# Gates of the recurrent mixer as two 64-row float32 products per unit

## The chip, the cores and the metric

The program runs on one core of one Trainium2 chip. The metric is the device time of one execution in microseconds, as the median of several executions. A profiled execution of the same program is read beside it: its span, from the first to the last instruction, and the instructions of the five engines (TensorE as PE, its weight loads as PEld, VectorE as DVE, ScalarE as ACT, GpSimd as POOL, and SyncE as SP, which here only issues transfers).

## What is computed

Two layers of a diffusion backbone with 256 latent tokens and 256 context tokens, 1024 wide. Each layer is a half-step SwiGLU block, a token mixer, and another half-step SwiGLU block, each behind an RMSNorm whose shift, scale and gate come from a conditioning vector. The change lies in the mixer. Its recurrent half has 8 heads of 64 channels, and its gates are block-diagonal products, one 64 by 64 matrix for each head, direction and kind:

```
def rglru_coeffs(xc, w_r, b_r, w_i, b_i, lam):
    xh = xc.reshape(bsz, n, LRU_HEADS, LRU_HEAD_DIM)
    r = jax.nn.sigmoid(jnp.einsum("bnhd,hde->bnhe", xh, w_r).reshape(bsz, n, LRU_WIDTH) + b_r)
    i = jax.nn.sigmoid(jnp.einsum("bnhd,hde->bnhe", xh, w_i).reshape(bsz, n, LRU_WIDTH) + b_i)
    log_a = (-RG_C * r * jax.nn.softplus(-lam)).astype(jnp.float32)
    a = jnp.exp(log_a)
    b = jnp.sqrt(-jnp.expm1(2.0 * log_a)) * (i * xc).astype(jnp.float32)
    return a, b
```

The scan `h = a * h + b` then runs forward and backward over latent and context tokens, and its sum is multiplied by a GELU branch. The other half of the mixer is a spatial gating block. Both halves feed one output projection.

## The kernel before

Channels lie on the 128 partitions and tokens on the free axis, 512 columns for both streams. The large weights come as 320 slots of 128 x 1024 float32 values through a ring of four slots (`raw`, `w_hi`, `w_lo`). ACT copies each slot into its rounded high part (`split_hi`, L877), DVE subtracts that from the original (`split_lo`, L1174), and PE makes three reduced-precision products for each block of 128 x 128 (`product`, L437): high by high, high by low, low by high. A slot q + 4 is split when slot q is done, so ACT and DVE have about three slots of room.

The mixer's `in_stage` has 16 slots, q = 0 to 15. Slots 0 to 3 give the recurrent input `xc` (ACT L1041, then a convolution on DVE, L1410), 4 to 7 the values of the spatial block (L718 to L720), 8 to 11 the GELU branch `gl`, 12 to 15 its multiplier. After each of the slots 3 to 10 PE computes one **unit** u = 0 to 7 of gates: channel tile t = u // 2 (two heads, 128 channels) and direction d = u % 2. A unit has two results in two banks of PSUM, for the kinds r and i.

The weights of a unit and a kind are a 128 x 128 matrix with two blocks of 64 x 64 on its diagonal and zeros elsewhere. They lie in `bd`, which is laid over the ring `ada_raw`, and POOL writes the zeros (`zero_blocks`). In layer 0 weights and `xc` are split in high and low parts as well: ACT L1035 and L1018, DVE L1553 and L1419, and PE makes three products for each kind (L747). In layer 1 PE takes the float32 operands as they are (L749), which the trace shows as two records for each product.

Behind a unit ACT reads the banks: a tanh of r into `l_q` (L1075), a tanh of i into `l_bx` (L1076, which signals `ti_ready`), an exponential into `l_a` (L1079) and a tanh into `l_s` (L1081). After units 3 and 7 it takes the square roots of four units (L1087), which needs another function table. DVE forms the coefficients (L1426, L1429) and after the roots the scans (L1438 to L1449). ACT may start unit 4 only when the first pair of scans is done, since `l_q` and the others have four buffers.

What orders the engines around it: PE's unit u waits for `ti_ready` of unit u - 1 in layer 0 (one pair of banks) and u - 2 in layer 1 (two pairs). Every engine runs its list in the order written, so a wait holds all that is queued behind it: on PE the next slots. The end of the mixer in layer 1 hangs on the last scans, on GELU (L1091), on the split of y (L1105, L1479), and on the output slots that take it.

## Time and profile before

| | us |
|---|---|
| median of 3 runs | 1577.48 |
| lowest and highest | 1576.68, 1584.05 |
| span of the profiled execution | 1575.5 |
| PE busy | 1561.2 (99%) |
| DVE busy | 1001.6 (64%) |
| ACT busy | 631.0 (40%) |
| POOL busy | 82.5 (5%) |

The median is 2.0 us above the profiled span. A busy share is a mean over stages; ACT at 40% is nearly full in one of them. Ends of matmuls are modelled, so the pace of PE is read from the starts of its records: the three-product stream of 512 columns has a start every 0.23 us.

### The profile page before, as it was taken

Reading aid. Unit: us, or ns where it says so; the run is one execution under the profiler, and the core shown is the slowest. Engines: PE = TensorE matmul, PEld = TensorE weight load, DVE = VectorE, ACT = ScalarE, POOL = GpSimd, SP = SyncE. Lnnn points to the kernel's source line nnn. Section 1 sums busy time; section 2 is a strip of 40 time slices with the busy share of each in tenths; the row PEclk is TensorE's granted clock in tenths of the full one; section 3 lists DMA queues with packets and bytes.
Section 4 is the critical chain, followed back from the end, with each engine's and each line's share of the span. In section 5 each row is a group of like instructions: output and inputs, shape, how many; then the busy total and the mean of one; then the engine's idle time right before and its main releaser. Section 6 shows DMA issues by size and latency. Waiting matters only on the chain.

```text
span 1575.5 us, 22302 instructions
## 1 busy us (share of the span) xinstructions
PE 1561.2 (99%) x9052; PEld 1338.1 (85%) x9052; DVE 1001.6 (64%) x1243; ACT 631.0 (40%) x856; POOL 82.5 (5%) x100
## 2 busy tenths in 40 slices
PE   8999999999999999999999999999999999999998
PEld 6888888888988888888888898888888897999998
DVE  5776773783967577777364267777445358975554
ACT  4433322332784343323222243333232249764553
POOL 0000000011100200000000100000000111000001
PEclk9999999999999999999999999999999999999999
DMA  9565553653322355565353336556354323456563
GB/s 365 201 197 179 186 162 119 208 192 94 115 75 79 94 166 193 176 201 173 107 196 99 107 121 201 193 183 195 100 173 148 107 91 108 147 188 197 190 203 117
DMA packets 71786, 249.95 MB, mean 159 GB/s; under 512 B 11664, under 2 KB 11920, under 8 KB 70672
## 3 DMA queue, kind: packets, MB, share of 16 engines
q1 hardware_dynamic: 71696, 248.70, 48.1%
q8 instruction: 62, 1.02, 0.3%
q14 instruction: 28, 0.23, 0.1%
HBM read 247.62 MB, written 1.05 MB: 158 GB/s over the span
## 4 chain that ended last, share of the span: by engine, by line
PE 96%; DVE 2%; ACT 1%; issue 0%; POOL 0%; POOLq 0%; DVEq 0%; ACTq 0%
PE bank L437 85%; PE bank L574 2%; PE bank L580 2%; PE bank L576 2%; PE bank L452 1%; PE bank L475 1%; PE bank L747 1%; PE bank L720 1%; PE bank L718 1%; PE bank L719 1%; PE bank L749 0%; PE bank L468 0%; DVE w_lo L1174 0%; PE bank L529 0%; PE bank L460 0%
## 5 line engine op out<-in xcount | busy, mean ns | idle before, releaser
L877 ACT ACTIVATE w_hi<-raw 128x1024 fp32r<-128x1024 f32 x317 | 335.9, 1060 | 807.0 <-PE bank L437 792.8
L1174 DVE TENSOR_TENSOR w_lo<-raw,w_hi 128x1024 fp32r<-128x1024 f32 x317 | 387.7, 1225 | 371.9 <-ACT w_hi L877 371.6
L437 PE MATMUL bank<-z_hi,w_hi 128*128 128x512 f32 (+1 forms) x1480 | 535.9, 362 | 2.4 <-DVE w_lo L1174 1.9
L437 PE MATMUL bank<-z_lo,w_hi 128*128 128x512 f32 (+1 forms) x1480 | 532.1, 360 | 0.0
L437 PE MATMUL bank<-z_hi,w_lo 128*128 128x512 f32 (+1 forms) x1480 | 531.9, 359 | 0.0
L437 PEld LDWEIGHTS bank<-z_hi,w_hi 128*128 128x128 f32 x1480 | 278.0, 188 | 49.7 <-DVE w_lo L1174 3.2
L437 PEld LDWEIGHTS bank<-z_hi,w_lo 128*128 128x128 f32 x1480 | 278.0, 188 | 42.6
L437 PEld LDWEIGHTS bank<-z_lo,w_hi 128*128 128x128 f32 x1480 | 278.1, 188 | 42.6 <-issue 1.0
L437 PE MATMUL bank<-h_hi,w_hi 128*128 128x512 f32 (+1 forms) x770 | 266.5, 346 | 0.0
L437 PE MATMUL bank<-h_lo,w_hi 128*128 128x512 f32 (+1 forms) x770 | 265.7, 345 | 0.0
L437 PE MATMUL bank<-h_hi,w_lo 128*128 128x512 f32 (+1 forms) x770 | 265.6, 345 | 0.0
L1349 DVE SCALAR_TENSOR_TENSOR up_acc<-ada_raw,c_cols,up_acc 128x1024 f32<-128x1024 f32 x168 | 208.0, 1280 | 3.5 <-ACT up_acc L977 2.4
L437 PEld LDWEIGHTS bank<-h_hi,w_hi 128*128 128x128 f32 x770 | 145.0, 188 | 19.3 <-issue 1.2
L437 PEld LDWEIGHTS bank<-h_hi,w_lo 128*128 128x128 f32 x770 | 145.0, 188 | 18.1
L437 PEld LDWEIGHTS bank<-h_lo,w_hi 128*128 128x128 f32 x770 | 145.1, 188 | 18.0
L1373 DVE TENSOR_TENSOR scr<-scr,bank 128x512 f32<-128x512 f32 (+1 forms) x88 | 54.6, 620 | 81.9 <-PE bank L437 81.6
L1701 POOL TENSOR_TENSOR scr<-scr 128x512 f32<-128x512 f32 (+1 forms) x29 | 47.6, 1641 | 776.0 <-ACT scr L891 776.0
L1187 DVE SCALAR_TENSOR_TENSOR res<-bank,gates,res 128x256 f32<-128x256 f32 x80 | 35.7, 479 | 66.1 <-PE bank L437 66.1
L1349 DVE SCALAR_TENSOR_TENSOR down_acc<-ada_raw,c_cols,down_acc 128x1024 f32<-128x1024 f32 x56 | 75.0, 1381 | 0.6 <-ACT down_acc L977 0.4
L925 ACT ACTIVATE z_hi<-scr,n_shift 128x256 fp32r<-128x256 f32 x88 | 42.8, 506 | 50.0 <-DVE scr L1273 50.0
L574 PE MATMUL bank<-z_hi,w_hi 128*128 128x256 f32 x208 | 56.4, 286 | 0.8 <-ACT z_hi L925 0.7
L576 PE MATMUL bank<-z_hi,w_lo 128*128 128x256 f32 x208 | 55.5, 282 | 0.0
(185 smaller groups left out, 1234.3 us busy)
## 6 DMA issues: line engine op xcount, KB each, us to landing
raw<-weights SPq DMA_DIRECT2D x320, 512.0 KB, 4.1
ada_raw<-ada_w SPq DMA_DIRECT2D x128, 512.0 KB, 4.2
ada_head<-head_w SPq DMA_DIRECT2D x8, 1024.0 KB, 18.5
res<-x_t SPq DMA_DIRECT2D x4, 512.0 KB, 4.8
ada_raw<-gate_w SPq DMA_DIRECT2D x4, 256.0 KB, 5.3
ws<-sgu_w SPq DMA_DIRECT2D x2, 256.0 KB, 4.0
bs<-sgu_b SPq DMA_DIRECT2D x2, 256.0 KB, 4.2
out<-final SPq DMA_DIRECT2D x2, 256.0 KB, 3.0
```

Of the source, the lines that this page charges most:

```text
L437: m = pe.matmul(bank[:, to], w, x[:, k, at], start=start and i == 0, stop=stop and i == 2, skip_group_check=True)
L452: m = pe.matmul(p_ada[32 * j:32 * j + 32, i * 256:i * 256 + 256], sel[:, st, :], w[:, st, :, j, :], start=(st == 0), stop=(st == 1), tile_ ...
L574: pe.matmul(banks[q][:, COLS[s]], w_hi[:, q, c], z_hi[:, k, z], start=(k == 0 and s == 0), stop=False, skip_group_check=True)
L576: pe.matmul(banks[q][:, COLS[s]], w_lo[:, q, c], z_hi[:, k, z], start=False, stop=False, skip_group_check=True)
L580: m = pe.matmul(banks[q][:, COLS[s]], w_hi[:, q, c], z_lo[:, k, z], start=False, stop=last, skip_group_check=True)
L877: act.activation(w_hi[:, r, :], raw[:, r, :], ACT.Copy).then_inc(hi_ready, 1)
L925: act.activation(z_hi[:, k, row_cols(n, s)], scr[:, k % 3, COLS[s]], ACT.Identity, bias=n_shift[:, n, k, s:s + 1]).then_inc(z_hi_ready, 1)
L1174: dve.tensor_tensor(w_lo[:, r, :], raw[:, r, :], w_hi[:, r, :].bitcast(F32), ALU.subtract).then_inc(lo_ready, 1)
L1187: m = dve.scalar_tensor_tensor(res[:, d, COLS[s]], tail_bank(d, s, n)[:, COLS[s]], gates[:, n - 1, d, s:s + 1], res[:, d, COLS[s]], ALU.mu ...
L1349: dve.scalar_tensor_tensor(acc[:, st, :], ada_raw[:, u % ADA_RING, :], c_cols[:, k, st:st + 1], acc[:, st, :], ALU.mult, ALU.add).then_inc ...
L1373: dve.tensor_tensor(scr[:, 2, 0:w], scr[:, q // 2, 0:w], pa[q][:, 0:w], ALU.mult).then_inc(hid_ready, 1)
L1701: pool.tensor_tensor(scr[:, 2, 0:w], scr[:, 2, 0:w], scr[:, d % 2, 0:w], ALU.add).then_inc(sqsum_ready, 1)
```

## The change

In both layers a unit's gates become two float32 products of 64 rows each. Each takes one head (64 of the 128 partitions of `xc`), and its 64 x 128 weights hold that head's r and i blocks side by side. The two products sit at row positions 0 and 64 of the array and write one bank each. The first bank then holds r of head 0 on partitions 0 to 63 and i on 64 to 127, the second i of head 1 on 0 to 63 and r on 64 to 127. So ACT reads each kind in two halves of 64 partitions: four tanh activations for a unit where there were two, with a third row of `half_b` for the shifted bias.

The splits of weights and of `xc` in layer 0, the zero blocks and their semaphores go. The weights come in four transfers for each layer in place of two, with the same bytes.

```
-                        if l == 0:
-                            pe.wait_ge(split_lo_ready, LT + t_ + 1)
-                        for kind_, dst in enumerate(gate_banks(l, u)):
-                            b = kind_ * 8 + d_ * 4 + t_
-                            if l == 0:
-                                for i, (w, x) in enumerate(((bd_high, xc_high), (bd_high, xc_low), (bd_low, xc_high))):
-                                    m = pe.matmul(dst[:], w[:, b, :], x[:, t_ % 2, :], start=(i == 0), stop=(i == 2))
-                            else:
-                                m = pe.matmul(dst[:], bd[:, b, :], xc[:, t_, :], start=True, stop=True)
+                        for a, dst in enumerate(gate_banks(l, u)):
+                            own = slice(64 * a, 64 * a + 64)
+                            m = pe.matmul(dst[:], bd[own, d_ * 4 + t_, :], xc[own, t_, :], start=True, stop=True,
+                                          tile_position=(64 * a, 0))
                         m.then_inc(gate_mm, 1)
...
-                        act.activation(l_q[:, r, :], g_r[:], ACT.Tanh, bias=half_b[:, 0, c:c + 1], scale=0.5).then_inc(act_chain, 1)
-                        act.activation(l_bx[:, r, :], g_i[:], ACT.Tanh, bias=half_b[:, 1, c:c + 1], scale=0.5).then_inc(ti_ready, 1)
+                        act.activation(l_q[low, r, :], first[low, :], ACT.Tanh, bias=half_b[low, 0, c:c + 1], scale=0.5)
+                        act.activation(l_q[high, r, :], second[high, :], ACT.Tanh, bias=half_b[high, 0, c:c + 1],
+                                       scale=0.5).then_inc(act_chain, 1)
+                        act.activation(l_bx[low, r, :], first[high, :], ACT.Tanh, bias=half_b[high, 2, c:c + 1], scale=0.5)
+                        act.activation(l_bx[high, r, :], second[low, :], ACT.Tanh, bias=half_b[low, 2, c:c + 1],
+                                       scale=0.5).then_inc(ti_ready, 1)
...
-                if l == 0:
-                    for t in range(LT):
-                        act.activation(bd_high[:, t::LT, :], bd[:, t::LT, :], ACT.Copy).then_inc(split_hi_ready, 1)
...
-            def gate_lo(t):
-                dve.tensor_tensor(xc_low[:, t % 2, :], xc[:, t, :], xc_high[:, t % 2, :].bitcast(F32),
-                                  ALU.subtract).then_inc(split_lo_ready, 1)
...
-                link(pool.memset(bd[0:64, :, 64:P], 0.0))
-                pool.memset(bd[64:P, :, 0:64], 0.0).then_inc(bd_zero, 1)
```

PE in layer 0, from the end of slot 3 over unit 0 into slot 4, before:

```order
1824 L437 MATMUL bank<-z_hi,w_lo 128x512
1825 L747 MATMUL bank<-xc_high,bd_high 128x512
1826 L747 MATMUL bank<-xc_low,bd_high 128x512
1827 L747 MATMUL bank<-xc_high,bd_low 128x512
1828 L747 MATMUL bank<-xc_high,bd_high 128x512
1829 L747 MATMUL bank<-xc_low,bd_high 128x512
1830 L747 MATMUL bank<-xc_high,bd_low 128x512
1831 L718 MATMUL bank<-w_hi,z_hi 128x512
```

The same place after the change (`ada_raw` is the tile over which `bd` lies):

```order
1824 L427 MATMUL bank<-z_hi,w_lo 128x512
1825 L732 MATMUL bank<-xc,ada_raw 128x512 x2
1826 L708 MATMUL bank<-w_hi,z_hi 128x512
1827 L709 MATMUL bank<-w_hi,z_lo 128x512
1828 L710 MATMUL bank<-w_lo,z_hi 128x512
```

Six products of a unit are now two, at the same place between the slots. In layer 1 there were two and are two.

ACT in layer 1, from slot 8's weight split over unit 4 to the start of unit 5, before:

```order
505 L877 ACTIVATE w_hi<-raw 128x1024
506 L1075 ACT_TABLE_LOAD
507 L1075 ACTIVATE l_q<-bank,half_b 128x512
508 L1076 ACTIVATE l_bx<-bank,half_b 128x512
509 L1079 ACTIVATE l_a<-l_q,lam_t 128x512
510 L1081 ACTIVATE l_s<-l_q,lam_t 128x512
511 L1048 ACTIVATE gl<-bank 128x256
512 L877 ACTIVATE w_hi<-raw 128x1024
513 L1060 ACTIVATE v_n<-bank,tok,tokr 128x512 x2
514 L1075 ACTIVATE l_q<-bank,half_b 128x512
```

And after:

```order
524 L861 ACTIVATE w_hi<-raw 128x1024
525 L1044 ACT_TABLE_LOAD
526 L1044 ACTIVATE l_q<-bank,half_b 64x512
527 L1045 ACTIVATE l_q<-bank,half_b 64x512
528 L1047 ACTIVATE l_bx<-bank,half_b 64x512
529 L1048 ACTIVATE l_bx<-bank,half_b 64x512
530 L1052 ACTIVATE l_a<-l_q,lam_t 128x512
531 L1054 ACTIVATE l_s<-l_q,lam_t 128x512
532 L1020 ACTIVATE gl<-bank 128x256
533 L861 ACTIVATE w_hi<-raw 128x1024
534 L1028 ACTIVATE v_n<-bank,tok,tokr 128x512 x2
535 L1044 ACTIVATE l_q<-bank,half_b 64x512
```

Each unit has two activations more on ACT, all four ahead of `ti_ready`; nothing else moved there.

## Rows read from the trace of the kernel before

**Rows 1.** The page: busy time, and the chain that ended last by engine.

```profile
PE 1561.2 (99%) x9052; PEld 1338.1 (85%) x9052; DVE 1001.6 (64%) x1243; ACT 631.0 (40%) x856; POOL 82.5 (5%) x100
...
PE 96%; DVE 2%; ACT 1%; issue 0%; POOL 0%; POOLq 0%; DVEq 0%; ACTq 0%
```

**Rows 2.** Chain in layer 1's mixer: start, length, what (us); a part of its pieces.

```profile
1319.72 1.73 PE bank L749 x4
1321.48 0.69 ACT l_q L1075
...
1347.70 1.28 ACT L1087
...
1358.04 4.22 PE bank L437 x31
```

**Rows 3.** PE's timeline: start, length, engine, line, operation, count; layer 0, unit 0.

```profile
419.68 0.39 PE L747 MATMUL bank<-xc_high,bd_high 128*128 128x512 f32 x1
...
421.06 0.39 PE L718 MATMUL bank<-w_hi,z_hi 128*128 128x512 f32 x1
```

**Rows 4.** PE's timeline, layer 1: units 0 and 6.

```profile
1306.10 1.88 PE L749 MATMUL bank<-xc,ada_raw 128*128 128x512 f32 x4
...
1308.05 0.40 PE L719 MATMUL bank<-w_hi,z_lo 128*128 128x512 f32 x1
...
1333.49 1.95 PE L749 MATMUL bank<-xc,ada_raw 128*128 128x512 f32 x4
```

**Rows 5.** PE's timeline around a sum that uses four column strips at once (L452).

```profile
142.99 0.39 PE L437 MATMUL bank<-z_hi,w_lo 128*128 128x512 f32 x1
143.31 1.93 PE L452 MATMUL bank<-up_acc,sel 128*32 128x256 f32 x32
...
145.51 0.40 PE L437 MATMUL bank<-z_lo,w_hi 128*128 128x512 f32 x1
```

**Rows 6.** The same line up to 143.35 and up to 143.65: count, ns, first to last start.

```profile
L452 PE MATMUL bank<-up_acc,sel x4: 403/403/403, 143.3 to 143.3; 128*32 128x256 f32 x4
...
L452 PE MATMUL bank<-up_acc,sel x8: 379/391/403, 143.3 to 143.6; 128*32 128x256 f32 x8
```

**Rows 7.** ACT's timeline, layer 1: unit 0, a wait, and unit 4.

```profile
1308.40 0.68 ACT L1075 ACTIVATE l_q<-bank,half_b 128x512 f32<-128x512 f32 x1
1308.97 0.70 ACT L1076 ACTIVATE l_bx<-bank,half_b 128x512 f32<-128x512 f32 x1
1309.54 0.83 ACT L1079 ACTIVATE l_a<-l_q,lam_t 128x512 f32<-128x512 f32 x1
1310.25 0.82 ACT L1081 ACTIVATE l_s<-l_q,lam_t 128x512 f32<-128x512 f32 x1
1310.96 1.06 ACT L877 ACTIVATE w_hi<-raw 128x1024 fp32r<-128x1024 f32 x1
1312.50 0.69 ACT L1075 ACTIVATE l_q<-bank,half_b 128x512 f32<-128x512 f32 x1 [0.49 <-PE bank L749]
...
1328.83 0.38 ACT L1048 ACTIVATE gl<-bank 128x256 f32<-128x256 f32 x1 [0.22 <-PE bank L437]
1329.11 1.05 ACT L877 ACTIVATE w_hi<-raw 128x1024 fp32r<-128x1024 f32 x1
```

**Rows 8.** ACT's timeline, layer 0: slot 6, units 3 and 4.

```profile
440.38 1.06 ACT L877 ACTIVATE w_hi<-raw 128x1024 fp32r<-128x1024 f32 x1 [2.69 <-PE bank L720]
441.76 0.69 ACT L1075 ACTIVATE l_q<-bank,half_b 128x512 f32<-128x512 f32 x1 [0.32 <-PE bank L747]
...
453.49 0.68 ACT L1076 ACTIVATE l_bx<-bank,half_b 128x512 f32<-128x512 f32 x1
```

**Rows 9.** Chain in layer 0's mixer: PE between slot 8 and unit 5.

```profile
454.26 1.63 PE bank L747 x6
```

**Rows 10.** Stretches at the end: busy PE, PEld, DVE, ACT, POOL, granted clock, DMA.

```profile
1571.00:1574.00 3.00, 0.00 (x0) 0.00 (x0) 0.45 (x1) 0.00 (x0) 0.81 (x1) 1.00 0.88 334
1574.00:1575.50 1.50, 0.00 (x0) 0.00 (x0) 0.00 (x0) 0.00 (x0) 0.00 (x0) 0.64 0.04 14
```

More of the change, by code:

```diff
@@ L47 @@
 GATE_LAG = 3
-GATE_HIGH_AT = (1, 2, 5, 7)
-GATE_LOW_AT = (0, 1, 5, 7)
 SIDE = 3
@@ L179, in build @@
         l_a = sb("l_a", [P, 4, T])
-        with ExitStack() as gate_scope:
-            sb("y_lru_first", [P, 2, T], F32, gate_scope)
-            xc_high = sb("xc_high", [P, 2, T], F32R, gate_scope)
         y_lru = sb("y_lru", [P, LT, T])
-        with ExitStack() as gate_scope:
-            sb("gl_first", [P, 2, T], F32, gate_scope)
-            xc_low = sb("xc_low", [P, 2, T], F32R, gate_scope)
         gl = sb("gl", [P, LT, T])
@@ L191, in build @@
         v_n = sb("v_n", [P, 4, 512])
-        with ExitStack() as gate_scope:
-            bd_high = sb("bd_high", [P, 16, P], F32R, gate_scope)
         y_sgu = sb("y_sgu", [P, LT, T])
@@ L196, in build @@
         xc = sb("xc", [P, LT, T])
-        bd_low = sb("bd_low", [P, 16, P], F32R)
+        sb("y_alone_rest", [P, 16, P])
         ws = sb("ws", [P, LT, P])
@@ L403, in _ @@
                             for a in range(2):
-                                sp.dma_start(bd[64 * a:64 * a + 64, :, 64 * a:64 * a + 64], gate_w[l, a]).then_inc(bd_in, 16)
+                                for kind in range(2):
+                                    c = 64 * (kind ^ a)
+                                    sp.dma_start(bd[64 * a:64 * a + 64, :, c:c + 64],
+                                                 gate_w[l, a][:, 8 * kind:8 * kind + 8, :]).then_inc(bd_in, 16)
                     if f == 0:
@@ L1011, in down_stage @@
                 norm(n, at["slot"] + DOWN_SLOTS)
-            def gate_hi(t):
-                if t >= 2:
-                    act.wait_ge(gate_mm, 2 * (t - 1))
-                act.wait_ge(xc_ready, t + 1)
-                act.activation(xc_high[:, t % 2, :], xc[:, t, :], ACT.Copy).then_inc(split_hi_ready, 1)
             def weight_ahead(slot, i):
@@ L1048, in in_stage @@
                         act.activation(gl[:, t, 0:wl], po[t % 2][:, 0:wl], ACT.Copy).then_inc(copy_ready, 1)
-                    if l == 0 and q == GATE_HIGH_AT[0]:
-                        gate_hi(0)
                     split_hi(at["slot"] + q + 4, q % 4)
-                    if l == 0 and q in GATE_HIGH_AT[1:]:
-                        gate_hi(GATE_HIGH_AT.index(q))
                     if q == 2:
@@ L1068, in in_stage @@
                         r = u % 4
-                        g_r, g_i = gate_banks(l, u)
+                        first, second = gate_banks(l, u)
+                        low, high = slice(0, 64), slice(64, P)
                         act.wait_ge(gate_mm, 8 * l + u + 1)
@@ L1549, in in_stage @@
                 m4 = wl // P
-                if l == 0:
-                    for t in range(LT):
-                        dve.wait_ge(split_hi_ready, t + 1)
-                        dve.tensor_tensor(bd_low[:, t::LT, :], bd[:, t::LT, :], bd_high[:, t::LT, :].bitcast(F32),
-                                          ALU.subtract).then_inc(split_lo_ready, 1)
                 for q in range(12):
@@ L1562, in in_stage @@
                     split_lo(s, q % 4)
-                    if l == 0 and q in GATE_LOW_AT:
-                        gate_lo(GATE_LOW_AT.index(q))
                     for u in {3: (0,), 4: (1,), 5: (2,), 6: (3,), 9: (4, 5), 10: (6,), 11: (7,)}.get(q, ()):
@@ L1640, in softplus @@
                 dve.tensor_scalar(half_b[:, 0, :], par[:, C_BR:C_BR + DEPTH * 2 * LT], 0.5, None, ALU.mult)
-                dve.tensor_scalar(half_b[:, 1, :], par[:, C_BI:C_BI + DEPTH * 2 * LT], 0.5, None, ALU.mult).then_inc(lam_ready, 1)
+                for a in range(2):
+                    of, to = slice(64 * a, 64 * a + 64), slice(64 - 64 * a, P - 64 * a)
+                    m = dve.tensor_scalar(half_b[to, 2, :], par[of, C_BI:C_BI + DEPTH * 2 * LT], 0.5, None, ALU.mult)
+                m.then_inc(lam_ready, 1)
             dve.memset(eps, EPS)
@@ L1754, in _ @@
                 norm(3 * l + 1)
-                zero_blocks(l)
+                zero_pads(l)
                 prep_gate(l, 1)
```

19 lines of the change are left out of this document (5 added, 14 removed).

## The prediction

> **What bounds the kernel now.** I read the page first: PE is busy 99% of the span and makes 96% of the chain that ended last [rows 1]. The reader should see that a stretch is in general worth what it takes on PE. Then I read the chain inside the two mixers, since the change lies only there. In layer 0 it is PE throughout, but for one short wait. In layer 1 it leaves PE: after unit 3 [rows 2] it runs over ACT and DVE (tanh, exponential, table load, scans), through units 5, 6 and 7 on ACT, over the last table load, until PE starts the output slots at 1358.04. From unit 3 on, layer 1's mixer is bound by ACT, and PE waits for it: unit 6 begins at 1333.49, only when unit 4's second tanh is read [rows 4]. So the change must be costed on two engines.
>
> **PE's part.** In layer 0 a unit takes six starts, 419.68 to 421.06: 1.38 us [rows 3]. In layer 1 it begins at 1306.10, and slot 4's second product begins at 1308.05; less the 0.23 us of its first that is 1.72 us, or 0.43 for each of four records [rows 4]. After the change both layers have two products of two records. If the two row positions run beside each other, that is 2 x 0.43 = 0.86 us.
>
> No row has row positions. The nearest are the sums over four column strips, also float32: four records start within 143.3, and the next four by 143.6, though each product has two records of its own [rows 6]. So strips do run beside each other, and products that are written one behind the other do not hold each other up. All 32 records and the way in and out take from 142.99 to 145.51, less two products of 0.23: 2.06 us [rows 5]. The strips' own pace is some 0.216 for four records, 8 x 0.216 = 1.73, so the change of shape costs 0.33 us for each visit. A gate's weights are four times wider than a strip's, and their load (an estimate: half of the 0.23 us pitch that a load and a product share in the stream, 0.11) is laid bare once more or not at all: a unit costs 0.86 + 0.33 to 0.44, and I take 1.25 us. The bounds are 0.86 (no cost of shape) and 1.72 + 0.4 = 2.1 (nothing beside anything). Against before that is -0.13 us for each unit in layer 0 and -0.47 in layer 1.
>
> By the Trainium skill, "TensorEngine Tiling (Array Packing)", Key Properties, a change of tiling mode drains TensorE; by that rule the 0.33 would be found here too, and rows 5 agree with it. "TensorE: Matmul & The Clock Gate", Part 3, The mechanism, speaks against this change in another way: products start and end in strict order. That is a rival below, worked out from rows.
>
> **ACT's part.** Each unit has two tanh activations more. Neighbouring ones of 128 x 512 start 0.57 us apart (1308.40, 1308.97, 1309.54), the exponential and the second tanh take 0.70 each [rows 7]. No row has 64 partitions. The lower bound is an activation with the same number of elements, 128 x 256, of which `gl` starts 0.28 ahead of the next [rows 7]; the upper bound is 0.57, where only columns count. I take 0.57, since the 512 columns stay and 128 partitions already run side by side. "ScalarE: Activation LUTs" of the Trainium skill gives one element per cycle and lane, so it too would leave the 0.57. A unit thus costs ACT 2 x 0.57 = 1.14 us more, all of it ahead of `ti_ready`, and behind it queue the exponential, the next weight split and the next unit.
>
> **Layer 1.** ACT needs 0.95 (weight split, 1310.96 to its successor) + 4 x 0.57 + 1.40 = 4.63 us for a unit; PE's period would fall from 4.49 to 4.02 us (2.77 for the slot plus 1.25). So ACT becomes the bound from unit 0 and PE's gain there is worth nothing. Walk ACT from 1308.40, where unit 0 starts as before. It has no wait left: unit 3, 3 x 4.64 later, starts at 1322.32, against 1321.48 [rows 2]; +0.84. Units 3 to 7 then add 5 x 1.14 = 5.70. All of the chain to 1358.04 hangs on that, except that ACT had waited 0.28 us for POOL's statistics ahead of unit 5, which now is ready first. Sum +6.26 us. DVE and the weights are not late: slot 15's high part would be made about 1350 and is wanted about 1359. PE would lie idle some 6 us ahead of unit 6 (due at 1330.5, released at 1336.6), 2 ahead of unit 7 and 2.7 ahead of the spatial products behind slot 12.
>
> That idle time could cost clock. At the end of this kernel PE has nothing from 1571 on, and the granted clock falls within 1574 to 1575.5 (0.64 there) [rows 10]. If it falls here, unit 6 and slot 10 at half pace take 8.3 us in place of 4.1 and end 2.1 us after the release of unit 7. ACT wants unit 7's gates only at 1350.1, some 5 us later, so I cost it at nothing; the cover is ACT's own lateness.
>
> **Layer 0.** ACT's 4.64 us a unit lie under PE's period of 6.8, with one exception. Units 4 to 7 reuse buffers, so between unit 3 and unit 5 the chain is: slot 6 done, unit 3 on ACT, table load, roots, scans, table load, unit 4's tanhs, then PE's unit 5. Before, unit 5 began at 454.26 [rows 9] with 0.41 us of wait (unit 4's second tanh began at 453.49 [rows 8]). Now unit 3's gates are ready 4 x 0.13 = 0.5 us earlier, and ACT, which had waited 0.32 for them behind its weight split [rows 8], starts earlier by as much. Units 3 and 4 add 1.14 each. Unit 5 begins at 454.26 - 0.5 + 2.28 = 456.04; PE was there at 453.2, so it waits 2.8 us. Units 5, 6 and 7 give back 3 x 0.13. Layer 0 ends +1.4 us; with units of 0.86 us it would be -0.8, with 2.1 us +7.4.
>
> **Edits that cost and bring nothing.** The eight weight and input splits on ACT and the eight on DVE lay ahead of unit 5's chain or beside PE's products; PE waited for none of them, and ACT, early once, waits for PE by unit 1. POOL's zeros were beside PE too. Eight weight transfers in place of four add two issues of about 0.4 us to SP's queue for each layer, ahead of a weight slot that is wanted a slot time (5 us) later. Without that cover they would cost under 1 us.
>
> **Sum.** 6.3 + 1.4 = 7.7 us, on a profiled span of 1575.5: 1583.2. The median was 2.0 above the span, so 1585.2 us, 0.49% above 1577.48. A measurement of this kernel tells about 0.5% (7.9 us) from no change, so the forecast sits on the bound itself.
>
> **Rivals.** *Strict order.* If the second product's first record waits for the first product's second, three passes replace two: 3 x 0.43 + 0.39 = 1.68 us. Layer 1 keeps its 6.3; in layer 0 unit 5's chain is late by 4 x 0.30 + 2.28 and three units add 0.9: +4.4. Total +10.7: 1588.2. Rows 6 speak against it.
>
> *Nothing beside anything.* Units of 2.1 us: +7.4 in layer 0, and in layer 1 a PE period of 4.87 us above ACT's makes unit 3 later by another 0.7: +6.9. Total +14.3: 1591.8. That would also be the change not doing what it says.
>
> *Free shape.* Units of 0.86: 6.3 - 0.8 = +5.5, 1583.0. Rows 5 speak against it.
>
> *Half activations cost half.* If 64 x 512 takes 0.28 us, ACT has nothing more to do. Then unit 3 starts 4 x 0.47 = 1.9 us early in layer 1, and layer 0 gains 0.5 + 3 x 0.13: -2.8 us, 1574.7. The sign turns at about 0.35 us for a half activation. Even with free shape it would be some -7. Nothing in the profile has this form.
>
> *Clock in layer 0.* If PE's wait of 2.8 us ahead of unit 5 lets the clock fall, what follows is PE-bound; a few us at half pace add about 3: 1588.2.
>
> **How the numbers follow.** Forecast 0.60 (its own range 1583.5 to 1587, from 1 us either way for the walk), strict order 0.10, nothing beside 0.10, free shape 0.10, half activations 0.06, clock 0.04. Predicted is the forecast, 1585.2. The range 1581.5 to 1591 leaves out the half activations and nothing beside (0.16). The forecast's 0.60 splits evenly at the bound of 7.9 us: within 0.5% are 0.30 of it, free shape and most of half activations, 0.45; slower is the other 0.30 with three rivals, 0.53; faster 0.02.
>
> **What would show it.** In the new trace: gate records in pairs that start together, two pairs 0.43 us apart, and a unit of 1.2 to 1.3 us; tanh rows of 0.57 pitch with 64 partitions; ACT without a wait from 1308 to the last roots in layer 1; PE idle about 6 us ahead of unit 6 and 2.8 ahead of layer 0's unit 5; the output slots of layer 1 beginning 7.7 us later in the span. A shorter half activation, or units 6 and 7 released on time, would make it wrong.

## The result, and the profile after

The changed kernel takes 1598.03 us (median of 4 runs, 1595.9 to 1602.72) where the kernel before takes 1577.51: 1.0121 times as long, 95% interval 1.0096 to 1.0146. The forecast was 1585.2 us, its range ended at 1591. The profiled execution has a span of 1597.0 us, 1.8 below its own time of 1598.8.

The page after, to set beside [rows 1]: busy time, and the chain that ended last by engine.

```profile
PE 1568.5 (98%) x9036; PEld 1335.8 (84%) x9036; DVE 997.8 (62%) x1236; ACT 651.0 (41%) x880; POOL 80.5 (5%) x96
...
PE 93%; ACT 4%; DVE 1%; DMA 1%; issue 1%; SPq 0%; POOLq 0%; DVEq 0%; ACTq 0%
```

ACT has 20 us more work, and its part of the chain has gone from 1% to 4%. PE's timeline in layer 0 (start, length, engine, line, operation, count), the answer to [rows 3]:

```profile
420.77 0.39 PE L427 MATMUL bank<-z_hi,w_lo 128*128 128x512 f32 x1
421.09 1.13 PE L732 MATMUL bank<-xc,ada_raw 64*128 64x512 f32 x4
422.15 0.50 PE L708 MATMUL bank<-w_hi,z_hi 128*128 128x512 f32 x1
422.48 0.39 PE L709 MATMUL bank<-w_hi,z_lo 128*128 128x512 f32 x1
```

From 420.77 to 422.48 less two products of 0.23 a unit takes 1.25 us, as forecast. Its records up to 421.5 and up to 422 (count, duration in ns, first and last start):

```profile
L732 PE MATMUL bank<-xc,ada_raw x2: 694/694/694, 421.1 to 421.1; 64*128 64x512 f32 x2
...
L732 PE MATMUL bank<-xc,ada_raw x4: 589/642/694, 421.1 to 421.6; 64*128 64x512 f32 x4
```

The first records of both products start together (0.006 us apart in the trace), and the second ones 0.53 us later. ACT's timeline of a unit in layer 1, the answer to [rows 7]:

```profile
1314.87 1.06 ACT L861 ACTIVATE w_hi<-raw 128x1024 fp32r<-128x1024 f32 x1
1315.82 0.67 ACT L1044 ACTIVATE l_q<-bank,half_b 64x512 f32<-64x512 f32 x1
1316.51 0.68 ACT L1045 ACTIVATE l_q<-bank,half_b 64x512 f32<-64x512 f32 x1
1317.21 0.68 ACT L1047 ACTIVATE l_bx<-bank,half_b 64x512 f32<-64x512 f32 x1
1317.91 0.68 ACT L1048 ACTIVATE l_bx<-bank,half_b 64x512 f32<-64x512 f32 x1
1318.62 0.81 ACT L1052 ACTIVATE l_a<-l_q,lam_t 128x512 f32<-128x512 f32 x1
```

The half tanhs start 0.70 us apart where whole ones start 0.57 apart. From the first tanh to the exponential 2.80 us pass, before 1.14: 1.66 more, not 1.14. PE then waits in layer 0 for unit 5 and in layer 1 for unit 6 (PE's timeline, with the idle time before a row and who ended it):

```profile
457.93 2.08 PE L732 MATMUL bank<-xc,ada_raw 64*128 64x512 f32 x4 [3.07 <-ACT l_bx L1048]
459.94 0.79 PE L427 MATMUL bank<-z_hi,w_hi 128*128 128x512 f32 x1
460.53 0.63 PE L427 MATMUL bank<-z_lo,w_hi 128*128 128x512 f32 x1
460.96 0.63 PE L427 MATMUL bank<-z_hi,w_lo 128*128 128x512 f32 x1
...
1346.49 2.08 PE L732 MATMUL bank<-xc,ada_raw 64*128 64x512 f32 x4 [8.06 <-ACT l_bx L1048]
```

Both times a unit takes 2.08 us, and in layer 0 the products behind it start 0.43 us apart in place of 0.23: TensorE is at its lower level, 1.2 GHz. The stretches (busy PE, PEld, DVE, ACT, POOL, granted clock, DMA) show the fall:

```profile
450.00:457.00 7.00, 4.86 (x22) 3.67 (x20) 6.90 (x10) 4.51 (x6) 0.00 (x0) 1.00 0.14 42
457.00:464.00 7.00, 6.07 (x14) 3.73 (x15) 6.21 (x12) 6.88 (x11) 3.62 (x4) 0.52 0.09 35
1338.00:1341.00 3.00, 0.43 (x4) 0.22 (x2) 2.90 (x5) 3.00 (x6) 0.00 (x0) 1.00 0.00 0
1341.00:1351.50 10.50, 5.01 (x18) 3.54 (x19) 10.29 (x16) 9.43 (x14) 4.08 (x6) 0.52 0.17 53
```

A third wait, of 3.7 us, stands ahead of the spatial products behind slot 12 of layer 1 (forecast: 2.7), and behind it the granted clock is 0.66 once more, from 1364 to 1369.

And there is a loss that no step of the prediction names. PE's main line in the last down stage, 1520 to 1560 us of each trace, before (L437) and after (L427): count, duration in ns, first and last start.

```profile
L437 PE MATMUL bank<-h_lo,w_hi x119: 276/276/276, 1519.8 to 1559.9; 128*128 128x256 f32 x119
```

```profile
L427 PE MATMUL bank<-h_hi,w_hi x99: 280/284/284, 1524.4 to 1559.6; 128*128 128x256 f32 x99
```

Before, 119 starts of one of the three kinds fill 40.1 us, one product every 0.1133 us. After, 99 fill 35.2 us (98 steps of three), one every 0.120.

Setting the k-th product of one trace against the k-th of the other shows where the time was lost. The table does that for all kernels of this study: how many us PE falls behind the kernel before in each stretch (named by the time in the trace of before; gate products and the throwaway ones of e6 left out).

| | to 100 | 100-405 | layer 0 mixer, 405-510 | 510-1305 | layer 1 mixer, 1305-1400 | 1400-end | all |
|---|---|---|---|---|---|---|---|
| after | 0.55 | 0.77 | 5.33 | 0.77 | 10.51 | 3.49 | 21.42 |
| e1 layout only | -0.22 | 0.78 | 0.23 | 0.75 | 0.10 | 3.49 | 5.13 |
| e2 old layout | -0.22 | 0.01 | 3.84 | -0.01 | 10.00 | 0.00 | 13.62 |
| e3 half tanhs | 0.23 | 0.00 | 5.59 | 0.01 | 11.30 | 0.00 | 17.13 |
| e4 whole tanhs | 0.52 | -0.01 | -1.24 | 0.00 | -2.05 | 0.00 | -2.78 |
| e5 halves by group | 1.02 | 0.00 | 2.93 | -0.02 | 9.36 | 6.52 | 19.81 |
| e6 kept busy | 1.58 | 0.00 | 2.40 | 0.03 | 10.05 | 0.00 | 14.06 |
| e7 column 96 | 1.02 | 0.77 | 0.25 | 0.76 | 0.31 | 5.02 | 8.13 |
| e8 shift 128 | -0.54 | 2.78 | 0.47 | 6.28 | -0.23 | 6.52 | 15.28 |
| e9 square tiles | -0.26 | 0.00 | 5.04 | 0.03 | 1.23 | 6.51 | 12.55 |
| e10 shift 256 | 1.56 | 0.00 | -0.03 | 0.01 | 0.14 | 6.52 | 8.20 |
| e11 by output | -0.19 | 0.00 | 2.41 | 0.05 | 10.44 | 0.00 | 12.71 |
| e12 four quarters | 0.54 | 0.00 | -1.55 | 0.01 | 2.83 | 0.00 | 1.83 |
| e13 layer 0 alone | 0.32 | 0.00 | -1.55 | 0.00 | 0.00 | 0.00 | -1.23 |
| e14 plus 2 units | 0.78 | 0.00 | -1.54 | 0.04 | -1.01 | 0.00 | -1.73 |
| e15 plus 4 units | 1.47 | 0.00 | -1.54 | 0.05 | -0.91 | 6.51 | 5.58 |

The first column is chance, the arrival of the first weights. On some chips part of the executions of every kernel, the kernel before too, run all 256-column products from 1400 on at 0.118 us and end 6.5 us later (the 6.5 in the last column); where a time below is called undisturbed, these are left out.

### The profile page after: what moved, and what is told of

The parts are those of the page before. It is cut to its first block, busy times and chain, and to the rows that moved or that the text cites. A ratio compares the mean times of both kernels' runs of the same rounds, so it can differ in the third digit from the quotient of the medians.

```text
span 1597.0 us, 22281 instructions
## 1 busy us (share of the span) xinstructions
PE 1568.5 (98%) x9036; PEld 1335.8 (84%) x9036; DVE 997.8 (62%) x1236; ACT 651.0 (41%) x880; POOL 80.5 (5%) x96
## 3 DMA queue, kind: packets, MB, share of 16 engines
q8 instruction: 62, 1.02, 0.3%
## 4 chain that ended last, share of the span: by engine, by line
PE 93%; ACT 4%; DVE 1%; DMA 1%; issue 1%; SPq 0%; POOLq 0%; DVEq 0%; ACTq 0%
PE bank L427 84%; PE bank L564 2%; PE bank L570 2%; PE bank L566 2%; DMA ada_head<-head_w 1%; PE bank L442 1%; ACT w_hi L861 1%; ACT l_q L1045 0%; PE bank L519 0%; ACT l_bx L1048 0%; ACT l_q L1044 0%; ACT l_a L1052 0%; PE bank L732 0%; PE bank L708 0%; PE bank L743 0%
## 5 line engine op out<-in xcount | busy, mean ns | idle before, releaser
L427 PE MATMUL bank<-z_hi,w_hi 128*128 128x512 f32 (+1 forms) x1480 | 538.4, 364 | 1.9 <-DVE w_lo L1147 1.4
L427 PE MATMUL bank<-z_lo,w_hi 128*128 128x512 f32 (+1 forms) x1480 | 535.2, 362 | 0.0
L427 PE MATMUL bank<-z_hi,w_lo 128*128 128x512 f32 (+1 forms) x1480 | 534.9, 361 | 0.0
L427 PEld LDWEIGHTS bank<-z_hi,w_hi 128*128 128x128 f32 x1480 | 280.4, 189 | 55.1 <-issue 10.2
L427 PEld LDWEIGHTS bank<-z_hi,w_lo 128*128 128x128 f32 x1480 | 280.1, 189 | 42.8
L427 PEld LDWEIGHTS bank<-z_lo,w_hi 128*128 128x128 f32 x1480 | 280.3, 189 | 41.5
L427 PE MATMUL bank<-h_hi,w_hi 128*128 128x512 f32 (+1 forms) x770 | 268.7, 349 | 0.0
L427 PE MATMUL bank<-h_hi,w_lo 128*128 128x512 f32 (+1 forms) x770 | 268.3, 348 | 0.0
L427 PE MATMUL bank<-h_lo,w_hi 128*128 128x512 f32 (+1 forms) x770 | 266.9, 347 | 0.0
L427 PEld LDWEIGHTS bank<-h_lo,w_hi 128*128 128x128 f32 x770 | 145.4, 189 | 19.6
L427 PEld LDWEIGHTS bank<-h_hi,w_hi 128*128 128x128 f32 x770 | 145.6, 189 | 19.2 <-issue 1.2
L427 PEld LDWEIGHTS bank<-h_hi,w_lo 128*128 128x128 f32 x770 | 145.5, 189 | 19.1
```

The costliest lines, as they stand in the source:

```text
L427: m = pe.matmul(bank[:, to], w, x[:, k, at], start=start and i == 0, stop=stop and i == 2, skip_group_check=True)
```

## Experiments

**e1 and e2: the layout.** The third row of `half_b` makes that tile 64 bytes longer in each partition, and all tiles allocated behind it (`h_hi`, `h_lo`, `y_hi` and the mixer's) stand 64 bytes further on. e1 puts that alone into the kernel before, e2 takes it alone out of the changed one.

```
-        half_b = sb("half_b", [P, 2, DEPTH * 2 * LT])
+        half_b = sb("half_b", [P, 3, DEPTH * 2 * LT])
```

> The kernel before with one row more in half_b (three in place of two, the third unused), as the change has it. Nothing else differs; every tile that is allocated behind half_b lies 64 bytes further on. Layout theory: the four down stages run at the slower pace seen in the changed kernel (256-column products every 0.120 us in place of 0.113 in the last one, 512-column ones every 0.229 in place of 0.227 in the other three), which is 528 products x 0.006 = 3.1 us plus some 0.8 for each of three: +5.5 us, 1583. Rival, that the pace came from the gates or from a fallen clock: no difference, 1577.5.

> The changed kernel, but the shifted bias goes to the unused row 1 of half_b, so that half_b keeps two rows and all tiles lie where they lay before. Layout theory: 5.5 us less than the changed kernel, about 1592.5, with 0.113 us between products in the last down stage. Rival: 1598 as the changed kernel, with 0.120 there.

e1 took 1583.09 us, 1.0033 times before (1.0021 to 1.0044), with nothing computed otherwise. e2 took 1591.41 (1.0084, 1.0067 to 1.0101). Last down stage of e1, same view as above:

```profile
L437 PE MATMUL bank<-h_hi,w_lo x112: 283/283/283, 1519.8 to 1559.8; 128*128 128x256 f32 x112
```

112 where 119 fitted. So 5.5 us of the loss are the layout: 3.5 in the last down stage, the rest nearly all in the three down stages of 512 columns, where a product takes 0.229 us in place of 0.227. (The 256-column products of those three stages give a little back: 0.115 to 0.117 in place of 0.119.) Only stages whose moving operand is a shifted tile are slower.

**e3 and e4: tanhs against products.** e3 has the kernel before's products and layout with each tanh in two halves. e4 is e2 with two whole tanhs; on half of the partitions it takes the one gate for the other, so its output isn't the reference's, but every engine has the instructions of the change with whole tanhs.

```
-                        act.activation(l_q[:, r, :], g_r[:], ACT.Tanh, bias=half_b[:, 0, c:c + 1], scale=0.5).then_inc(act_chain, 1)
...
+                        for to, bank, row, ready in ((l_q, g_r, 0, act_chain), (l_bx, g_i, 1, ti_ready)):
+                            for a in range(2):
+                                own = slice(64 * a, 64 * a + 64)
+                                m = act.activation(to[own, r, :], bank[own, :], ACT.Tanh, bias=half_b[own, row, c:c + 1],
+                                                   scale=0.5)
+                            m.then_inc(ready, 1)
```

> The kernel before (products, splits and layout as before) with each of a unit's two tanhs made in two halves of 64 partitions, the same partitions in bank and tile. If a half takes 0.70 us from start to start wherever it reads, as in the changed kernel, a unit costs ACT 1.66 us more: in layer 1 unit 3 starts 2.4 us late and five units add 8.3, +10.5 us; in layer 0 units 3 and 4 add 3.3, and a wait of that length may cost clock, up to 3.4 more: 1591 to 1595. Rival, that 0.70 belongs to reading the banks of row products or to crossing partitions, and a plain half takes 0.57: +1.14 a unit, some +8.5 us, 1586.

> The changed kernel in the old layout, with the two tanhs of a unit taken over all 128 partitions, the first bank to l_q and the second to l_bx. It leaves out the sorting of r and i by head, so the gates are mixed up; every other instruction is there. It is the products' part alone. My walk says: units of 1.25 us, layer 1's chain starts 1.9 us early and layer 0 gains 0.9: -2.7 us, 1574.8, and the clock never falls in the mixers. Rival, that the 64-row products cost something beyond their own time: 1577.5 or more.

e3: 1594.3 us (1.0101, 1.0084 to 1.0118). e4: 1574.25 (0.9977, 0.9967 to 0.9987). The halves alone cost 16.7 us; the products alone bring 3.4. Both signs are thus shown apart: the edit that the change is named after is a gain, what it forces on ACT is five times that.

**e5 and e11: why 0.70.** e5 is e3 with the four halves ordered by partitions, `l_q` low, `l_bx` low, `l_q` high, `l_bx` high. e11 puts the same order of outputs into e2, where the two kinds of one head come from opposite halves of a bank.

> The kernel before with its own gate products and layout, and each tanh in two halves of 64 partitions, now ordered by partitions: l_q low, l_bx low, l_q high, l_bx high. So of the two steps between neighbouring halves of a unit that e3 had from low to high, and the one back, the middle one is now the only change of partitions; the steps from a half to the next on the same 64 partitions are two. Theory A (any ScalarE activation on 64 partitions costs 0.70 us, as the 0.70 between starts in e3): the starts stay 0.70 us apart everywhere and the time is that of e3, 1594.3 +- 1.5 us. Theory B (the 0.13 us over the 0.57 of a whole tanh come from the change of partitions): two of the four starts are 0.57 us apart, a unit costs about 0.26 us less in ScalarE, 8 units of layer 1 save 2.1 us, and the time is about 1592; if the write of one half is also what the next waits for, more.

> e2 (the change with the old layout) with the four half tanhs of a unit in another order: l_q low, l_bx low, l_q high, l_bx high, by the partitions that they write. Within each pair the tanh reads the other 64 partitions than the one ahead of it, but writes the same; between the pairs it reads the same and writes others. Theory A (the 0.12 us on top of a start come where the written partitions change, as in e5 from low to high): two of the four distances are 0.57 us, 8 units of layer 1 save 2 us, 1589 us. Theory B (they come where the partitions that are read change): only the middle distance and none of the pairs' is 0.57 us, about 1 us saved, 1590.4. Theory C (where either changes): 0.70 everywhere, 1591.4 as e2. Nothing is left out.

ACT's timeline in layer 1, e5 and then e11:

```profile
1317.37 0.69 ACT L1077 ACTIVATE l_q<-bank,half_b 64x512 f32<-64x512 f32 x1
1317.96 0.67 ACT L1080 ACTIVATE l_bx<-bank,half_b 64x512 f32<-64x512 f32 x1
1318.64 0.68 ACT L1077 ACTIVATE l_q<-bank,half_b 64x512 f32<-64x512 f32 x1
1319.23 0.67 ACT L1080 ACTIVATE l_bx<-bank,half_b 64x512 f32<-64x512 f32 x1
1319.92 0.81 ACT L1085 ACTIVATE l_a<-l_q,lam_t 128x512 f32<-128x512 f32 x1
```

```profile
1315.86 0.67 ACT L1044 ACTIVATE l_q<-bank,half_b 64x512 f32<-64x512 f32 x1
1316.54 0.69 ACT L1045 ACTIVATE l_bx<-bank,half_b 64x512 f32<-64x512 f32 x1
1317.23 0.68 ACT L1046 ACTIVATE l_q<-bank,half_b 64x512 f32<-64x512 f32 x1
1317.94 0.68 ACT L1048 ACTIVATE l_bx<-bank,half_b 64x512 f32<-64x512 f32 x1
1318.65 0.82 ACT L1052 ACTIVATE l_a<-l_q,lam_t 128x512 f32<-128x512 f32 x1
```

In e5 the distances are 0.59, 0.68, 0.59, 0.69: a half costs nearly what a whole one costs (0.57) when it follows one on the same partitions, and 0.1 us more when the partitions change. In e11 the second half writes the same partitions as the first and reads others: 0.68. The third writes others: 0.69. So a change on either side is enough, theory C. In layer 1's mixer e5 loses 9.36 us where e3 loses 11.30, close to the 2.1 that theory B of e5 expected. e5 took 1590.6 us undisturbed (four runs, 1588.8 to 1592.8), e3 1594.3, of which a part is a fall of the clock in layer 0 that e5's trace does not have. Two runs of e11, the profiled one first, took 1590.1 and 1590.9, like e2; the other two took 1594.4 and 1599.4, and without their traces it stays open what they lost. "VectorE: DVE Perf Modes" of the Trainium skill, section "Two Vector instructions with no wait between them", has this rule for VectorE: an instruction is held until all earlier ones have finished when an input or the output starts in another group of 32 partitions than the last one's. These rows show the same pattern on ScalarE (0.59 against 0.68), and every half tanh of the change but the first of a unit is such a case.

The traces of e3 and e5 show one case more. The last half of a unit there reads the high partitions of a bank and the next unit's first half the low ones. Three activations lie between them, but none reads a bank. The distance from the weight split to that first half is 1.07 us (in e3 from 1318.47 to 1319.54), where the change, whose last half reads low partitions, has 0.95 (1320.04 to 1320.99). So what was read from the banks last counts, even with reads of other memory in between. Each of e3's units takes 5.31 us in place of 5.17, which is why its layer 1 costs 11.3 us and not 10.5.

**e6: the clock.** e2 with throwaway products where PE waits: two ahead of unit 5 in layer 0, six ahead of unit 6 and three ahead of the spatial products in layer 1.

```
+                            if (l, u) == (0, 5):
+                                pe.wait_ge(copy_ready, 8 * l + 4)
+                                throwaway(2, po[1], T)
...
+                                throwaway(6, po[0], T)
```

> e2 (the change with its third row of half_b put back into the second, so the old layout) and throwaway products of full precision, 128x512, about 0.86 us each in the rows of before, whose results nothing reads: 2 ahead of unit 5 of layer 0's mixer, 6 ahead of unit 6 and 3 ahead of the spatial products of layer 1's mixer, where TensorE stood waiting in e2 (about 3, 8 and 4 us). Nothing of the computation is left out. Theory A (the clock's fall after those waits costs what the slow products of layer 0 are longer by, about 0.2 us for each product over 3.4 to 6.8 us, and nearly nothing in layer 1, where ScalarE sets the pace): no stretch of the mixers at the lower clock, 1.5 to 3 us less than e2, 1588.4 to 1590. Theory B (the falls hide beside ScalarE's work in both layers): 1591.4, as e2. Theory C (the falls cost their whole length, 17 us at half speed): 1583.

Stretches of e2, then of e6 (busy PE, PEld, DVE, ACT, POOL, granted clock, DMA):

```profile
456.30:459.70 3.40, 3.30 (x7) 1.63 (x8) 3.30 (x5) 3.40 (x5) 3.15 (x4) 0.51 0.01 2
1337.00:1347.00 10.00, 4.31 (x15) 2.83 (x15) 9.79 (x15) 8.95 (x13) 4.08 (x6) 0.50 0.18 54
```

```profile
455.00:460.00 5.00, 3.73 (x13) 1.53 (x12) 4.90 (x13) 4.91 (x9) 1.96 (x2) 1.00 0.28 107
1335.00:1345.00 10.00, 7.41 (x24) 3.43 (x24) 9.73 (x15) 8.95 (x14) 3.24 (x5) 1.00 0.17 54
```

The falls at both waits are gone (a shorter one stands behind unit 7: 0.54 from 1350 to 1353.5). By the table, layer 0's mixer costs 2.40 us in place of 3.84, and layer 1's the same 10.0. e11, whose ACT work in layer 0 is e2's and whose clock happened not to fall there, has 2.41. So in layer 0 a fall of 3.4 us costs 1.4; in layer 1 taking 10 us of the lower clock away changed nothing that can be seen, since ACT sets the pace. Even the lower clock behind the spatial products is covered: e2 has it from about 1361, e6 does not, but e6 then waits 1.0 us for DVE's split of y, which hangs on ACT's last roots. The time itself, 1591.0 us undisturbed (four runs, 1589.9 to 1591.8) against e2's 1591.4, is too coarse for it and misses the 1588.4 to 1590 of theory A: its profiled run also lost 1.6 us in the head.

**e7, e8, e10: what of the layout.** In the built program of the kernel before `h_hi` starts at byte 137,856 of a partition and `z_hi` at 32,896, both a multiple of 128 but not of 256. The 256-column stages from 1400 on start at column 112, 64 bytes past a multiple of 128. e7 has e1's shift and starts at column 96; e8 shifts by 128 bytes, e10 by 256.

> The kernel before with the third row of half_b (64 bytes a partition, as in e1) and with the first column of the lone 256-column sequence put from 112 to 96, that is 64 bytes earlier: so the numbers that TensorE reads as moving columns in the last down stage stand where they stood before the shift, while all other tiles stand as in e1. Theory A (where the moving columns start sets the pace of a 256-column product): the last down stage runs at 0.113 us a product again and not at 0.120, about 3 us less than e1, 1580 us. Theory B (the place of the weights or of something else sets it): 0.120 stays, 1583.1. The 512-column down stages stay at 0.229 either way.

> The kernel before with two rows more in half_b, so that every tile behind it stands 128 bytes later and not 64 as in e1. If only the place modulo 128 bytes matters, the paces are those of before, 0.227 and 0.1133 us, and the time is 1577.6 +- 0.5. If a shift costs by its size or by a larger period, they are others: 1583 or more, or less than before if the layout of before is not the best one.

> The kernel before with four rows more in half_b: every tile behind it stands 256 bytes later. e1 (64 bytes) had 0.229 and 0.120 us a product in the down stages and e8 (128 bytes) 0.229 to 0.237. Theory A (the place modulo 256 bytes decides): the paces of before, 0.227 and 0.1133 us, 1577.6 +- 0.5 us. Theory B (a larger period, or the distance to the weights): slower down stages again, 1580 or more.

The last down stage of e7:

```profile
L437 PE MATMUL bank<-h_lo,w_hi x119: 276/276/276, 1519.8 to 1559.9; 128*128 128x256 f32 x119
```

119 again, as before: where the moving columns start sets the pace (theory A). The time I expected, 1580, did not come, since column 96 puts the other operand, `z_hi`, on a multiple of 128, and the stage that reads it from 1395 to 1506, which had 0.1133, now takes 0.119 a product: 5.0 us, and e7 is at 1584.7 undisturbed (five runs, 1584.3 to 1585.5). e8 expected the layout of before to come back at 128 bytes; it didn't. Its down stage of layer 0, 315 to 345, beside that of before:

```profile
L437 PE MATMUL bank<-h_hi,w_hi x44: 392/395/398, 314.7 to 344.8; 128*128 128x512 f32 x44
```

```profile
L437 PE MATMUL bank<-h_hi,w_hi x45: 389/389/389, 314.7 to 344.6; 128*128 128x512 f32 x45
```

e8 took 1592.58 us (1.0073, 1.0049 to 1.0097), and 1588.8 to 1589.6 in its three undisturbed runs, some 12 us above before. With 256 bytes, e10, the pace is back in the 512-column stages (the table has 0.0 in the three stretches that hold them), and the five undisturbed runs lie at 1577.0 to 1578.05, as before. So the pace of the 512-column products returns when the address moves by 256 bytes and not when it moves by 64 or 128. The profiled runs of e8 and e10 are disturbed ones, so their 256-column pace from 1400 on can't be told, and why 128 bytes cost more than 64 in the 512-column stages stays open.

**e9 and e12: the products with whole tanhs.** Both cut the product in two along the columns, so that each gate lands in a bank of its own.

```
-  m = pe.matmul(dst[:], bd[own, d_ * 4 + t_, :], xc[own, t_, :], start=True, stop=True, tile_position=(64 * a, 0))
+  m = pe.matmul(dst[own, :], bd[own, d_ * 4 + t_, c:c + 64], xc[own, t_, :], ..., tile_position=(64 * a, 64 * a))
```

> The change with each of its products cut in two along the columns of the array: four full-precision products of 64 rows by 64 columns a unit, head a of gate k on rows and columns 64a to 64a+63, so that each gate's two heads land in one bank, on the partitions where the kernel before had them. The two whole tanhs of 128 partitions stay, the bias needs no shifted copy, and the layout is that of before. Nothing is left out. Theory A (products on other rows and other columns run beside each other as those of after did, two starts 0.01 us apart and the next pair 0.53 us later): a unit's products take 1.25 us on TensorE, as in e4, and the time is e4's, 1574.3 +- 0.6 us, 3.3 us less than before. Theory B (products of 64 columns do not run beside each other): four starts 0.5 us apart, about 1.06 us more for each of 16 units, 1585 to 1591. Theory C (all four products of a unit are in flight together): up to 0.5 us less for each of the 8 units of layer 0, 1570.

e9: 1583.8 us undisturbed (seven runs, 1583.15 to 1584.23). Its theory A overlooked that the second gate of a head would need the same quarter as the first. The records, line L734 from 419.0 to 419.9 and then to 421:

```profile
L734 PE MATMUL bank<-xc,ada_raw x2: 640/640/640, 419.5 to 419.5; 64*64 64x512 f32 x2
...
L734 PE MATMUL bank<-xc,ada_raw x8: 589/589/640, 419.5 to 420.9; 64*64 64x512 f32 x8
```

Two start together, and the eight records take four steps. e12 gives each of the four its own quarter; the input gate's heads then lie crosswise, and DVE's first coefficient operation is cut in two.

```
+                            for a in range(2):
+                                own, to_ = slice(64 * a, 64 * a + 64), 64 * (kind_ ^ a)
+                                m = pe.matmul(dst[to_:to_ + 64, :], bd[own, d_ * 4 + t_, to_:to_ + 64], xc[own, t_, :],
+                                              start=True, stop=True, tile_position=(64 * a, to_))
...
+                    m = dve.scalar_tensor_tensor(l_bx[own, r, :], ti[other, r, :], 1.0, xc[own, u // 2, :], ALU.add, ALU.mult)
```

> As e9, four full-precision products of 64 rows by 64 columns a unit, but each on its own quarter of the array: head a's recurrence gate on rows and columns 64a, its input gate on rows 64a and the other 64 columns, so that the input gate's bank holds the two heads the other way round. The tanhs are the two whole ones of 128 partitions, and the product of the input gate with xc, on VectorE, becomes two operations of 64 partitions that read the heads crosswise: one more operation of about 0.6 us on VectorE for each of 16 units. Layout of before, nothing left out. In e9 the pairs ran beside each other and the two pairs on the same quarters one after the other (starts 419.51, 419.99, 420.42, 420.84: 1.86 us a unit). Theory A (all four run together, since each has its own quarter): the starts of a unit fall into two groups 0.53 us apart, 1.25 us a unit as in after, ScalarE as before; the time is e4's 1574.3 plus what VectorE's added 5 us in layer 1 put on the path, 0 to 3 us: 1575.5. Theory B (only two run together): as e9, 1583.8, plus VectorE's.

Line L733 of e12, 419.0 to 420.5 and to 421.5:

```profile
L733 PE MATMUL bank<-xc,ada_raw x4: 640/640/640, 420.3 to 420.3; 64*64 64x512 f32 x4
...
L733 PE MATMUL bank<-xc,ada_raw x8: 589/614/640, 420.3 to 420.8; 64*64 64x512 f32 x8
```

PE's timeline at its longest wait in layer 1 (ahead of the output slots), DVE's timeline there, and a stretch (busy PE, PEld, DVE, ...):

```profile
1358.24 0.56 PE L427 MATMUL bank<-y_hi_alone,w_hi 128*128 128x256 f32 x1 [3.29 <-DVE y_lo_alone L1446]
1358.60 0.42 PE L427 MATMUL bank<-y_lo_alone,w_hi 128*128 128x256 f32 x1
1358.81 0.41 PE L427 MATMUL bank<-y_hi_alone,w_lo 128*128 128x256 f32 x1
...
1363.89 0.28 PE L427 MATMUL bank<-y_hi_alone,w_lo 128*128 128x256 f32 x1
```

```profile
1318.61 1.39 DVE L1392 SCALAR_TENSOR_TENSOR l_bx<-ti,xc 64x512 f32<-64x512 f32 x2
1320.03 0.69 DVE L1396 SCALAR_TENSOR_TENSOR l_q<-l_a,l_bx 128x512 f32<-128x512 f32 x1
```

```profile
1330.00:1350.00 20.00, 16.88 (x136) 14.91 (x137) 19.40 (x29) 19.80 (x31) 4.08 (x6) 1.00 0.41 132
```

All four run together. Layer 0's mixer gains 1.55 us. In layer 1 PE is 3.0 us earlier by 1333, but eight crossed pairs of 1.39 us in place of 0.69 are 5.6 us more for a DVE that is busy 19.4 of 20 us there, and the mixer ends 2.8 late. Only part of that is DVE's work itself: the output slots start 1.2 us late, and then the granted clock is 0.50 up to 1363.8 (products 0.21 us apart in place of 0.11), behind a wait of 3.3 us where the kernel before waits 1.0. That brings the other 1.6. The time is 1579.15 (1.0013, 1.0000 to 1.0025) where 1575.5 was expected: on PE a gain, in all none.

**e13, e14, e15: the same where DVE has room.** e13 has the crossed form in layer 0 and the kernel before's in layer 1; e14 adds units 0 and 1 of layer 1, e15 units 0 to 3.

```
+        def crossed(l, u):
+            return l == 0 or u < 2
```

> e12's four products on four quarters and its crossed VectorE operations in layer 0 alone; layer 1 has the kernel before's two full-precision products of 128 rows with zero blocks, whole tanhs and one VectorE operation. Layout of before, nothing left out. In e12's trace the products of layer 0 stood 1.54 us earlier after the mixer than ahead of it, against before, and it lost 2.8 us in layer 1, where VectorE's added 5.6 us ended last. Theory A (what a gate product's new form is worth depends on the engine that has room: in layer 0 TensorE sets the pace and VectorE has room, 24 of 35 us busy in e4): -1.5 us, kept to the end, 1576.1 where the kernel before has 1577.6. Theory B (layer 0's gain is given back in the stages behind it): 1577.6.

> e13 and, in layer 1, the crossed form for units 0 and 1 too (two crossed VectorE operations, 1.4 us in all, and about 0.5 us less on TensorE for each unit). Nothing left out. Theory A (layer 1 ends by VectorE, which in e12 gave back all but 0.8 us of its added 5.6 us): 0.6 us more than e13, 1576.7. Theory B (layer 1 ends by TensorE and ScalarE as long as VectorE's addition is small): up to 1 us less than e13, 1575.1.

> e14 with the crossed form for units 0 to 3 of layer 1: two more units on TensorE at 0.5 us less each, two more VectorE operations of 0.7 us. Nothing left out. e14 kept its whole 1.0 us for two units, e12 (all eight units) gave back 5 us at the end of the mixer, to VectorE. Theory A (VectorE's row of work has some 2.5 us to spare up to the middle of the mixer): another 1.0 us, 1574.5. Theory B (VectorE has no more to spare than the 0.8 us worked out from e12): its four added operations of 2.8 us are late by 2 us at the end, 1576.5.

e13: 1576.47 us (0.9990, 0.9981 to 0.9998), its 1.55 us kept to the end. e14: 1575.47 (0.9985, 0.9974 to 0.9996), another 1.0. It leaves nothing out and is the fastest such kernel here, 2.1 us under before. e15 brings nothing more: 1575.7 undisturbed (six runs, 1575.36 to 1576.27). PE has gained 2.0 us by unit 5 of layer 1 and waits twice for ACT after it:

```profile
1332.39 1.96 PE L745 MATMUL bank<-xc,ada_raw 128*128 128x512 f32 x4 [1.06 <-ACT l_bx L1063]
...
1337.77 1.96 PE L745 MATMUL bank<-xc,ada_raw 128*128 128x512 f32 x4 [0.56 <-ACT l_bx L1063]
```

So past two units the products' gain meets ACT, as the prediction's walk had it, not DVE as theory B of e15 had it. Theory A of e14 and theory B of e15 took all of e12's loss for DVE's work, and 1.6 us of it were the clock. The output slots of e14 and e15 wait 1.1 us for DVE, as in the kernel before (1.0), so it is the crossed units behind the fourth that made e12's long wait.

## Why the prediction was wrong, and where it was right

**The half tanh: the step that failed.** The prediction bounded it by 0.28 and 0.57 us and took "the upper bound is 0.57, where only columns count". It is 0.70, outside the bounds: the rows behind the bound all had neighbours on the same partitions. So the term of 1.14 us a unit on ACT measured 1.66. Everything that hangs on it keeps its form. Walking layer 1 again with 1.66 in place of 1.14 (a unit of 5.17 us on ACT): unit 3 starts at 1308.40 + 3 x 5.17 = 1323.91, 2.4 later than before; five units add 8.3; less 0.28: +10.5. Measured: 10.5 in the change, 10.0 to 10.4 in e2, e6 and e11 (and 11.3 in e3, whose units take 5.31). The same in layer 0: 1.4 + 2 x 0.52 = 2.4; measured 2.4 where the clock did not fall. With that one number the forecast would have been 12.9 us and not 7.7, a time of 1590.4. That would still lie in the range, if barely; the two parts below carried the time out of it.

**The layout: a part that the sum did not have.** Under the edits that "cost and bring nothing" the third row of `half_b` does not even stand. It cost 5.5 us (e1), more than the 4.2 us by which the forecast was short in layer 1. So it is a term that the prediction had at nothing without a reason. No row of the trace of before could price it, but the edit was in the diff, and an unknown of this kind belonged in the range.

**The clock in layer 0.** It stood as a rival with +3 us and 0.04. It happened: in the profiled run the lower clock covered 6.8 us, and layer 0's mixer cost 5.3 us, of which 2.4 are ACT and 0.2 the layout (e1), so 2.7 us. The price was right, the chance far too low; of the five kernels with half tanhs of 0.70 us on every step (after, e2, e3, e6, e11), three had the fall, one had its cause filled up and one escaped it. In layer 1 the prediction costed the fall at nothing, and e6 bears that out.

**What held.** Units of 1.25 us. The surcharge over 2 x 0.43 was taken as 0.33 to 0.44, with the 0.33 from the shape in [rows 5], and is 0.39: about 0.1 each at the way in and the way out, and 0.1 in each of the two steps. Products in pairs beside each other, so strict order and nothing beside anything fell; free shape fell too (by the prediction's own formula its layer 0 is 2.28 - 7 x 0.52 = -1.4 and not -0.8, which touches neither forecast nor range). ACT without a wait in layer 1 but the one for the scans, PE waiting ahead of unit 5 in layer 0 and ahead of unit 6 in layer 1 (8 us where 6 were forecast; ahead of unit 7, at the lower clock, hardly any of the 2). The products' own worth, -0.13 us a unit in layer 0 and -0.47 in layer 1: e4, with whole tanhs, has -1.2 and -2.0 in the two mixers, in layer 1 the worth of four units before ACT sets the pace. The median lies only 1.0 us above the profiled span, where 2.0 was added.

The whole of the 21.4 us in the profiled run is then 10.5 + 2.4 for ACT, 2.7 for the clock, 5.3 for the layout and 0.5 of chance in the head. Against the forecast's 7.7 that is 5.2 more for the half tanhs, 2.7 for the clock and 5.3 for the layout.

## What to carry to other kernels

A ScalarE instruction cut in two by partitions cost as much as two whole ones here, and 0.1 us more for each neighbour on other partitions, so a gain on one engine that changes where results land must be priced on the engine that reads them. A tile made longer moves every tile behind it: keep the moving operand's address modulo 256 bytes, or measure the moved layout alone, before judging an edit. And a new form is worth most where the engine that pays for it has room: here in layer 0 and in two units of layer 1, 2.1 us, where eight units in both layers gave nothing. A longer wait can cost twice: once as a wait, and once by the clock behind it, if TensorE sets the pace there (1.6 us in e12, 2.7 in the change).

## What the runs showed of the hardware that was not expected

ScalarE starts activations of 64 partitions and 512 columns 0.59 us apart on the same partitions and 0.70 apart when the partitions read or written change. For reads of a bank the last read of a bank counts, even with other activations in between (0.95 us against 1.07 in e3).

TensorE's float32r products of 256 columns took 0.1133 us with the moving operand 64 bytes past a multiple of 128 and 0.119 to 0.120 on a multiple. (The ones that e1 moves from a multiple to 64 bytes past it took 0.115 to 0.117.) Those of 512 columns 0.227 on an odd multiple of 128 (`h_hi` at 137,856), 0.229 with 64 bytes more, up to 0.237 with 128 more, and 0.227 again with 256 more.

Four float32 products on the four quarters of the array started together (420.3), with two of different rows writing different partitions of one bank at the same time, and the kernel still computes its function. "TensorEngine Tiling (Array Packing)" of the Trainium skill, Gotcha 1, says that different row tiles can't access the same bank at once; e9 and e12 did so in every unit, on different partitions of the bank, so here the measurement decides. Nothing here shows two row tiles on the same partitions.
